# The low parts of six weight chunks made by GpSimd between the decay levels of the first block

## The reference

```
proj = rmsnorm(x) @ w_in            # 1024 x 2832
o_a = gated linear attention, decay f = lb + (1-lb) * sigmoid(.)
o_b = conv(4 taps) -> gates r, gi -> h_t = a_t h_(t-1) + u_t, times gelu(.)
o_c = gated linear attention, decay from log_sigmoid(.) / 16
x = x + concat(o_a, o_b, o_c) @ w_out
x = x + (gelu(conv(h @ w_gate)) * (h @ w_val)) @ w_down
```

## Time and profile before

| what | value |
|---|---|
| median of 3 runs | 1544.21 us (1543.34 to 1546.0) |
| profiled execution | 1546.39 us |
| its span | 1545.1 us |
| mean granted clock of TensorE | 0.938 |
| busy: TensorE, VectorE, ScalarE, GpSimd | 92%, 56%, 44%, 6% |
| instructions | 23177 |

### The profile page before, as it was taken

The page is one execution under the profiler, slowest core; times in us unless marked ns, Lnnn a source line. Parts: engine busy times, 40 slices in busy tenths (PEclk is TensorE's granted clock), DMA queues, the critical chain, the costliest instruction groups (busy, mean ns, idle before and its releaser), DMA issues.

```text
span 1545.1 us, 23177 instructions
## 1 busy us (share of the span) xinstructions
PE 1427.2 (92%) x9749; PEld 1302.2 (84%) x9750; DVE 866.6 (56%) x1175; ACT 681.0 (44%) x982; POOL 97.1 (6%) x138
## 2 busy tenths in 40 slices
PE   4899799999999998898899999999998898999997
PEld 4788799988899998766889999899988756889997
DVE  4687656657545464454754456545564454655555
ACT  4456344544434443445344443444433444344432
POOL 1133000000000000250000000000000250000000
PEclk9898889999999999968999999999999767999999
DMA  5333266766565653500565566665653500465651
GB/s 164 108 108 123 82 204 191 225 182 191 165 201 180 186 169 97 183 1 1 146 197 185 180 182 183 189 194 173 183 162 110 171 0 1 137 210 172 191 183 64
DMA packets 294672, 230.79 MB, mean 149 GB/s; under 512 B 10139, under 2 KB 277290, under 8 KB 294314
## 3 DMA queue, kind: packets, MB, share of 16 engines
q1 hardware_dynamic: 294554, 229.31, 48.6%
q10 hardware_dynamic: 16, 0.00, 0.0%
HBM read 228.24 MB, written 1.05 MB: 148 GB/s over the span
## 4 chain that ended last, share of the span: by engine, by line
PE 77%; DVE 13%; ACT 6%; DMA 2%; issue 2%; SPq 0%; DVEq 0%; ACTq 0%
PE bank L726 22%; PE bank L727 22%; PE bank L728 22%; PE bank L1073 3%; DVE lo_gu L1497 3%; PE bank L1103 3%; ACT hi_gu L1152 2%; PE bank L1090 1%; PE bank L736 1%; PE bank L1034 1%; PE bank L928 1%; DMA st_gu<-in_ffn_w_gu 1%; DMA st_gu<-in_ffn_w_val 1%; DVE stats L1524 1%; PE bank L938 1%
## 5 line engine op out<-in xcount | busy, mean ns | idle before, releaser
L726 PE MATMUL bank<-xTh,hi_gu 128*128 128x256 f32 x1736 | 495.6, 285 | 8.3 <-DVE big L1701 5.8
L727 PE MATMUL bank<-xTl,hi_gu 128*128 128x256 f32 x1736 | 494.8, 285 | 0.0
L728 PE MATMUL bank<-xTh,lo_gu 128*128 128x256 f32 x1736 | 494.7, 285 | 0.0
L1497 DVE TENSOR_TENSOR lo_gu<-st_gu,hi_gu 128x2048 fp32r<-128x2048 f32 (+1 forms) x140 | 317.4, 2268 | 224.4 <-ACT hi_gu L1152 224.4
L726 PEld LDWEIGHTS bank<-xTh,hi_gu 128*128 128x128 f32 x1736 | 337.0, 194 | 11.6 <-issue 7.2
L727 PEld LDWEIGHTS bank<-xTl,hi_gu 128*128 128x128 f32 x1736 | 336.9, 194 | 1.7
L728 PEld LDWEIGHTS bank<-xTh,lo_gu 128*128 128x128 f32 x1736 | 336.8, 194 | 0.0
L1152 ACT ACTIVATE hi_gu<-st_gu 128x2048 fp32r<-128x2048 f32 (+2 forms) x145 | 273.0, 1883 | 39.8 <-DMA st_gu<-in_ffn_w_gu 19.1
L726 PE MATMUL bank<-hi_dn,actTh 128*128 128x512 f32 x436 | 171.7, 394 | 10.8 <-DVE actTl L1630 7.4
L726 PE MATMUL bank<-hi_gu,xTh 128*128 128x256 f32 (+1 forms) x576 | 168.6, 293 | 13.9 <-DVE xTl L1512 9.4
L727 PE MATMUL bank<-lo_dn,actTh 128*128 128x512 f32 x436 | 170.3, 391 | 0.0
(11 more groups left out here) (262 smaller groups left out, 1536.8 us busy)
## 6 DMA issues: line engine op xcount, KB each, us to landing
st_gu<-in_ffn_w_gu SPq DMA_DIRECT2D x176, 512.0 KB, 5.1
st_dn<-in_ffn_w_down SPq DMA_DIRECT2D x109, 512.0 KB, 6.4
st_gu<-in_w_in SPq DMA_DIRECT2D x27, 1024.0 KB, 5.5
st_gu<-in_w_out SPq DMA_DIRECT2D x12, 1024.0 KB, 5.2
st_gu<-in_ffn_w_gate SPq DMA_DIRECT2D x21, 512.0 KB, 5.1
st_gu<-in_ffn_w_val SPq DMA_DIRECT2D x21, 512.0 KB, 6.4
gb<-in_ln_g SPq DMA_DIRECT2D x6, 512.0 KB, 7.0
gb<-in_ln_b SPq DMA_DIRECT2D x6, 512.0 KB, 8.1
```

Of the source, the lines that this page charges most:

```text
L726: pe.matmul(o, lhs[0], rhs[0], start=start, stop=False, **kw)
L727: pe.matmul(o, lhs[0], rhs[1], start=False, stop=False, **kw)
L728: return pe.matmul(o, lhs[1], rhs[0], start=False, stop=stop, **kw)
L1497: dve.tensor_tensor(split_view(low_of(c), c), split_view(st_gu[c % 2], c), split_view(high_of(c), c).bitcast(F32), ALU.subtract).then_inc( ...
```

## The change

Chunks 6 to 11 are added to `low_by_pool`. VectorE's `weights_low` returns at once for them, and TensorE and SP wait on GpSimd's semaphore. In GpSimd's loop over the levels, `weights_low(lev + 4)` is added behind `k_factors(lev)` for levels 2 to 7, so chunks 6 to 11, one a level. In level 6 it stands ahead of L656. Nothing else is changed.

```diff
-        low_by_pool = {CHUNK_NO["t", 0, 0], *(CHUNK_NO["out2", l, j] for l in range(LAYERS) for j in range(2))}
+        low_by_pool = {CHUNK_NO["t", 0, 0], *(c for c in range(6, 12)), *(CHUNK_NO["out2", l, j] for l in range(LAYERS) for j in range(2))}
...
             for lev in range(1, LEV_N):
                 k_factors(lev)
+                if lev >= 2 and lev + 4 < 12:
+                    weights_low(lev + 4)
                 if lev == 6:
                     pool.wait_ge(lru_gate_ok.sem, lru_gate_ok[1, 1])
                     pool.tensor_tensor(gi, gi, xc, ALU.mult).then_inc(lru_gx.sem, lru_gx.one(0))
```

## The result

The changed kernel takes 1553.51 us, the median of 6 runs (1551.11 to 1554.45), against 1544.63 before (1543.34 to 1546.69). The ratio is 1.0054, with a 95% interval of 1.0041 to 1.0067: slower; the medians differ by 8.9 us. The forecast was 1554.4. The profiled execution took 1553.65 us, with a span of 1552.3.

The account below looks back on a forecast made before the run. TensorE was taken to pace the kernel. Chunk steps 0.5 + 1.8 + 1.8 + 0 + 2.8 + 2.3 = 9.2 us, plus 1.0 for TensorE's clock, gave 1544.2 + 10.2 = 1554.4 us; range 1549.0 to 1559.0.

Parts of the forecast that it names:

- the clock: TensorE falling to 1.2 GHz behind longer waits in the decay levels: 0 to 2 us, taken as +1.0.
- the port: VectorE operations with two SBUF inputs and GpSimd products or differences exclude each other, first asker first; holds up to 4.50 us.
- the queue: Work behind a low part on GpSimd comes late, above all gated product L656 behind chunk 10's: +2.8 us.
- TensorE paces, little can be won: In the first block's decay levels, even freeing VectorE entirely could give back only about 2 us.
- The rival of the other order at the port: GpSimd's low parts of chunks 6 and 9 go ahead of VectorE's subtraction L1723: +12.5, 1556.7 us; chance 18%.
- Chunk 6, +0.5: VectorE's L1729 is held to 78.65 against 78.13, +0.5 us; TensorE's 2.0 us wait for the chunk doesn't add.
- Chunks 7 and 8, +1.8 each: The convolution's first L1759 waits for GpSimd's low part: 4.50 - 2.29 - 0.4 = +1.8 us in each level.
- Chunk 9, 0: VectorE's L1723 asks first, then only selects from PSUM follow, so the move costs 0.
- Chunk 10, +2.8: Gated product L656 stands behind the low part on GpSimd, delaying ScalarE's exponentials L1341 and level 6's scores: +2.8 us.
- Chunk 11, +2.3: The second recurrence operation L1797 waits for GpSimd's low part, delaying L1723 and level 7's scores: +2.3 us.
- The delay is passed on whole: Behind level 7, head outputs, their norm and the output product follow in order, so the levels' delay reaches the end.

Follow-up runs that it names:

- Without the six low parts: Kernel before, with the low parts of chunks 6 to 11 computed by no engine and high parts waited for instead; 1542.88 us against 1544.73, ratio 0.9994.
- chunk 9 alone: Kernel before, with only chunk 9's low part moved to GpSimd and the other five left on VectorE; run once, 1545.3 us against 1545.38.
- two sources: Low parts of chunks 6 to 11 left out; GpSimd does unneeded scratch subtractions with inputs from two buffers in their places; 1554.45 us against 1544.41, ratio 1.0068.
- chunk 10 alone: Kernel before, with only chunk 10's low part moved to GpSimd and the other five left on VectorE; run once, 1548.23 us against 1545.38.
- the product first: Changed kernel, with GpSimd's gated product L656 put ahead of chunk 10's low part in level 6; 1552.19 us against 1544.73 for the kernel before, ratio 1.0049.
- memsets: Low parts of chunks 6 to 11 left out; GpSimd does three scratch memsets of 1610 elements at each place; 1547.71 us against 1544.73, ratio 1.0017.
- chunk 11 alone: Kernel before, with only chunk 11's low part moved to GpSimd and the other five left on VectorE; run once, 1551.58 us against 1545.38.

## Why the prediction was right

The forecast was +10.2, of which 9.2 from the two engines and 1.0 from the clock. The levels came to +10.6 in the profiled execution, 9.0 of it from the port and the queue and 1.6 from the clock, and the whole to +8.9. The mechanism is the forecast one; that the sum is met to about 1 us owes something to luck, since the clock term was too small, the whole was less than the levels, and the three executions behind the 1544.2 lay 0.4 us below the six. By its steps:

- **TensorE paces, little can be won** (about 2 us at most): right, even less. Without the six low parts 1.2 us came in the levels.
- **The port excludes, first come first served**: right between an operation with two inputs and a low part (a memset and L1760 above didn't keep to that order). L1761 waited 4.2 us, L1799 4.3, and L1725 went ahead of chunks 6, 9 and 10 in 0.98 to 1.00 us, as the first L1799 did ahead of chunk 11. The rival of the other order at the port, which hung on 0.15 us, did not come in any of the five kernels with such a low part or subtraction at chunk 6 or 9. Its price in the prediction doesn't add up either: 9.2 and 1.7 are 10.9, not 11.3, and with 1.0 for the clock 11.9, not 12.5.
- **Chunk 6, +0.5**: L1731 ended at 79.03, 0.3 earlier than expected counted from level 1, so +0.2. TensorE's wait was 1.85 against 2.0.
- **Chunks 7 and 8, +1.8 each**: measured +1.9 each. The L1725 at 101.71 is 4.07 us later than before counted from level 1; 4.1 was forecast. The amount is right, a reason in it is not. I had L1755, with one input in SBUF, run beside GpSimd. It didn't: it was issued 0.1 us earlier and went first. In the changed kernel GpSimd's low part, issued at 80.71, ends at 85.44, and that is 4.46 us, its own time, behind the end of L1757 at 80.98. So the 0.4 us that I took off for it wasn't there to take. But L1761 waited 4.2 us and not 4.5, and 4.2 less the 2.3 of VectorE's own low part is the measured 1.9.
- **Chunk 9, 0**: right, with chunk 9 alone, to 0.03.
- **Chunk 10, +2.8**: right. From level 4 to level 6 it was +2.74, +2.73 and +2.73 in the changed kernel, with two sources and with chunk 10 alone, and in the kernel with the product first ScalarE's wait for it is gone.
- **Chunk 11, +2.3**: +2.07 alone. TensorE's own waits for the low parts of chunks 8 and 11 were 0.93 and 0.32 instead of 2.3 and 1.7, because its scores ran slowly in front of them.
- **The clock, +1.0**: this term was mis-sized; it came to about 1.6. I priced a fall at 1.5 us for a chunk; it slows the scores too and costs 2.9 where it is uncovered. In the changed kernel most was covered by waits for the port, as I had argued: 0.6 us showed at level 4 and about 1 at level 7 (VectorE's last select ended at 144.2, TensorE began the scores at 145.33). The two overlap: between levels 6 and 7 the clock alone costs 2.9 (chunk 10 alone, memsets), the port alone 2.1 (chunk 11 alone), and both together 3.1. And the fall isn't set by the wait alone, as the last section shows.
- **The delay is passed on whole**: over the kernels with several executions the whole follows the levels within 1.7 us, in the profiled execution not. From level 7 to the deviation of the last norm it took 1396.4 us after and 1399.5 before. In the nine experiments that stretch took 1395.6 to 1399.8, and the delay of the levels doesn't order it: 1399.8 with the product first, 1395.9 with two sources, 1396.4 without the low parts. I take these 4 us for chance, which one profile of each kernel can't show, and the profiled execution of before was at the slow end. A part of it is visible. The first 14 us of the output product had a mean clock of 0.79 before and 0.87 after:

```profile
162.00:176.00 14.00, 13.99 (x95) 13.99 (x96) 7.00 (x4) 6.29 (x4) 0.00 (x0) 0.79 0.71 199
```

```profile
172.00:186.00 14.00, 14.00 (x104) 14.00 (x105) 7.12 (x4) 6.18 (x5) 0.00 (x0) 0.87 0.73 207
```

The rest of this scatter I haven't traced.

The Trainium skill (SBUF — State Buffer, section "SBUF: two separate sides") names the pair of ports as an exclusive lock that a VectorE operation with two SBUF inputs contends for only against a GpSimd operation that reads SBUF. The runs agree: L1764 waited 4.2 us for the subtraction with two sources and not at all for the memsets. The memsets' hold on L1760, 1.71 us instead of 0.40, fits its statement that the pair is one of read and write ports, if L1760 runs in one of the two-port modes; no run here shows which mode it was in.

## What to carry to other kernels

Before work is moved from VectorE to GpSimd, look in the trace for a tiny VectorE operation with two SBUF inputs that takes as long as the GpSimd operation beside it; where there is one, ask what VectorE does next. Of the six moves here none gained; the one that cost nothing (chunk 9) had VectorE reading PSUM or waiting for others beside it. Look also at what stands behind the moved instruction on GpSimd's queue: a product with 0.35 us of lead cost 2.8 us. And leave the work out altogether once, for a ceiling, before a better place for it is sought: here that was 1.2 us.

## What the runs showed of the hardware

- GpSimd's subtraction of 128 x 2048 takes 0.9 us less when both inputs are the same buffer (3.73 against 4.67 us at the same place of two otherwise equal kernels).
- A GpSimd memset holds up a VectorE operation with one SBUF input (L1760: 1.54 to 1.71 us instead of 0.40, four times of four) and lets one with two pass (L1764: 1.53 for three, as before).
- TensorE's clock doesn't follow the wait in front of it in any simple way. At 2.4 GHz it went through waits of 1.67 us (level 1) and 1.85 us (chunk 6) in the changed kernel. It fell to 1.2 GHz after 1.67 us at level 1 with chunk 11 alone, and after 1.77 (memsets), 2.04 and 2.64. In the kernel with the product first it fell after 1.90 us at chunk 6 and stayed over 1.92 us at the gates. In the changed kernel it also fell in the middle of the scores of level 3, behind a wait of only 0.43:

```profile
96.00:98.00 2.00, 1.81 (x16) 1.15 (x14) 2.00 (x1) 0.00 (x0) 2.00 (x1) 0.77 0.00 0
98.00:100.00 2.00, 1.27 (x6) 1.30 (x7) 1.93 (x4) 0.00 (x0) 0.59 (x1) 0.50 0.12 13
```

So a wait near 2 us before the scores is a risk, not a price: from nothing to 2.9 us in a level, and 4.4 in one kernel (chunk 11 alone, level 1).
